# A fused two-block kernel: six modulation products moved among a filter's eight tap steps, and a modulation's row turned between the next step's two products

## The reference, cut to what matters

```
# first block
mod = silu(c) @ mod_w + mod_b                   # 12 pieces of 512 columns
u = a * sigmoid(gt)                             # from h @ w1 + b1
u = causal_dwconv(u, dw_w) + dw_b               # 31 taps, depthwise, 8 tiles of 128 channels
u = silu(layernorm(u)); y = u @ w2 + b2
# second block, needs nothing of the first: its two filters
h = (hdn @ fw3 + fb3).reshape(L, 2, 2, 512)     # hdn: 1024 x 64
h = h * exp(-t * deltas)
hk = rfft(concat([h_fwd, 0, h_bwd reversed]))   # as a product with a table "filt"
```

## Time and profile before

| | |
|---|---|
| median of 3 runs | 3297.73 us (3294.17 to 3299.56) |
| the profiled execution | 3292.07 us, its span 3290.3 us |
| PE busy | 3096.4 us, 94% of the span |
| DVE busy | 1712.3 us, 52% |
| ACT, POOL busy | 1011.6 us, 399.8 us |
| stretch of the list `OTHER` | about 245 to 464 us of the span |

### The profile page before, as it was taken

The page is one execution under the profiler, slowest core; times in us unless marked ns, Lnnn a source line. Parts: engine busy times, 40 slices in busy tenths (PEclk is TensorE's granted clock), DMA queues, the critical chain, the costliest instruction groups (busy, mean ns, idle before and its releaser), DMA issues. The chain is left out here.

```text
span 3290.3 us, 33491 instructions
## 1 busy us (share of the span) xinstructions
PE 3096.4 (94%) x13786; PEld 2499.5 (76%) x13786; DVE 1712.3 (52%) x1776; ACT 1011.6 (31%) x1203; POOL 399.8 (12%) x161
## 2 busy tenths in 40 slices
PE   7998869899999999989999999899999999999996
PEld 3784357788888888778888877677877788888885
DVE  5697786656556554574511076577455322223225
ACT  3454444332222122233221133476222311111111
POOL 0595550000000000000200034000110000000000
PEclk9998879899999999899999999999998999999998
DMA  6114423132223331321432343531331202112112
GB/s 207 58 33 159 148 96 113 73 109 64 90 77 116 100 100 63 109 77 64 141 113 92 108 154 128 136 74 50 126 118 56 76 26 64 49 38 62 38 45 109
DMA packets 96192, 301.24 MB, mean 92 GB/s; under 512 B 11205, under 2 KB 15045, under 8 KB 95847
## 3 DMA queue, kind: packets, MB, share of 16 engines
q1 hardware_dynamic: 96040, 299.09, 27.8%
HBM read 251.34 MB, written 47.71 MB: 91 GB/s over the span
## 5 line engine op out<-in xcount | busy, mean ns | idle before, releaser
L708 PE MATMUL ps<-mainr,wh 128*128 128x512 f32 (+1 forms) x6592 | 1782.0, 390 | 29.5 <-issue 12.7
L708 PEld LDWEIGHTS ps<-mainr,wh 128*128 128x128 f32 x6592 | 1238.6, 189 | 286.6 <-issue 31.2
L708 PE MATMUL ps<-mainr,wl 128*128 128x512 f32 (+1 forms) x3296 | 1030.7, 389 | 0.0
L708 PEld LDWEIGHTS ps<-mainr,wl 128*128 128x128 f32 x3296 | 623.1, 189 | 128.6
L1713 DVE TENSOR_TENSOR wl<-raw,wh 128x1024 fp32r<-128x1024 f32 (+2 forms) x272 | 294.1, 1083 | 457.1 <-ACT wh L1235 456.9
L1235 ACT CAST wh<-raw 128x1024 fp32r<-128x1024 f32 (+2 forms) x320 | 282.0, 886 | 746.9 <-PE ps L708 538.3
L1972 DVE TENSOR_TENSOR mainf<-mainf,ps 128x1024 f32<-128x1024 f32 x80 | 97.7, 1221 | 215.0 <-PE ps L708 215.0
L754 PE MATMUL ps<-mainr,wh 128*128 128x512 f32 x576 | 164.4, 409 | 36.0 <-issue 21.8
L2013 DVE SCALAR_TENSOR_TENSOR ps<-mainf,vec,ps 128x1024 f32<-128x1024 f32 (+1 forms) x174 | 180.9, 1102 | 2.5 <-ACT ps L1424 2.3
L2497 POOL TENSOR_TENSOR tmp<-tmp,mainf 128x1024 f32<-128x1024 f32 x8 | 27.5, 3444 | 1160.6 <-DMA mainf<-in_rope 1097.5
L1049 PE MATMUL ps<-mainr,wh 128*128 128x512 f32 x512 | 160.3, 395 | 6.3 <-POOL wl L2464 6.1
(11 more groups left out here) (236 smaller groups left out, 2896.8 us busy)
## 6 DMA issues: line engine op xcount, KB each, us to landing
raw<-in_mod_w SPq DMA_DIRECT2D x48, 512.0 KB, 4.5
raw<-in_ada_w SPq DMA_DIRECT2D x48, 512.0 KB, 3.7
raw<-in_f_up SPq DMA_DIRECT2D x44, 512.0 KB, 4.2
raw<-in_g_up SPq DMA_DIRECT2D x44, 512.0 KB, 3.5
raw<-in_w_in SPq DMA_DIRECT2D x40, 512.0 KB, 4.1
raw<-in_pw SPq DMA_DIRECT2D x24, 512.0 KB, 3.6
sc_x<-mainf SPq DMA_DIRECT2D x24, 512.0 KB, 2.6
mainf<-sc_x SPq DMA_DIRECT2D x24, 512.0 KB, 6.2
```

What stands on the lines that cost most here:

```text
L708: ins = e.matmul(out, wt[:, a:b], xs[n], start=kk == 0 and t == 0, stop=kk == kt - 1 and t == 2)
```

## The change

In the list, the modulation pieces come behind steps 0, 3 and 5 of each filter instead of 3, 5 and 7. On PE and DVE, the turn and the bias add are done inside the next tap step: between the products of its two banks, and between the two "dec". Nothing is added or taken away.

```diff
     for s in range(32):
         out.append(("f", s))
-        if s % 16 < 8 and s % 2 == 1 and s not in (1, 17):
+        if s % 16 in (0, 3, 5):
             out.append(next(mods))
...
-    def filter_step(s):
+    def filter_step(s, turn):
...
                 e.matmul(k.BANK("taps", o, step, n), m.ex[0:65, 128 * step:128 * step + 128],
                          m.mf[0:65, 3 * SLOT + c0:3 * SLOT + c0 + 512], start=True, stop=True).then_inc(*k.to("taps", o, step, n))
+                if turn and n == 0:
+                    modulation_turn(*turn)
...
     for kind, s in OTHER:
-        if turn:
-            modulation_turn(*turn)
+        if kind == "f":
+            filter_step(s, turn)
             turn = None
-        if kind == "f":
-            filter_step(s)
...
                 e.tensor_tensor(t, t, dec, ALU.mult).then_inc(*k.to("dec", o, step, n))
+                if row and n == 0:
+                    modulation_add(*row)
...
     for kind, s in OTHER:
-        if row:
-            modulation_add(*row)
+        if kind == "f":
+            filter_step(s, row)
             row = None
-        if kind == "f":
-            filter_step(s)
```

More of the change, by code:

```diff
@@ L2041, in filter_pairs, with filter_step @@
         e.scalar_tensor_tensor(out=b, in0=b, scalar=-2.0, in1=f, op0=ALU.mult, op1=ALU.add).then_inc(*k.to("fw3d", 1))
-    def filter_step(s):
+    def filter_step(s, row):
         o, step = s // 16, s % 16
```

## The result

The changed kernel took 3281.99 us (median of 10 runs, 3277.29 to 3293.38), the kernel before, beside it, 3293.82 us (10 runs, 3290.13 to 3299.56). The ratio is 0.9964 [0.9956, 0.9972]: 11.9 us faster, with an interval of 9 to 14.5. The forecast of 3282.5 holds, and the likeliest case came true. The sum behind it was 15.2 us.

What follows compares the result with a forecast made beforehand. DVE was taken to bound the kernel through its waits before 410; gains of 6.2 us (first filter) and 9.0 (second) sum to 15.2, giving 3282.5 from the median 3297.7. Range 3276 to 3296, the forecast's own 3278 to 3288.

Steps and rivals of the forecast that it cites:

- the likeliest case: Whole kernel: 15.2 us less waiting, to 3282.5 us from the median; chance 70%.
- DVE is what bounds the stretch: In the list, DVE sets the length: each microsecond of its waiting removed before 410 should shorten the kernel.
- no change: Rival: product steps or POOL's additions set both filters' time, so waits only change place: 3297; chance 9%.
- the slower one: Rival: half clock stays through all modulations, 14.1 us each; 16 us slower than before, about 3313; chance 9%.
- part of the gain is lost: Rival: closer packing brings more slow DVE splits beside POOL, 6.3 us in one filter, about 3289; chance 12%.
- The product step moves off the path: First filter: first product step runs beside DVE's steps 6 and 7, ending 301.5 at half clock against 307.0 before.
- First modulation, step 0: First filter, behind step 0: length 8.9 us, step 1's convolution at 259.2 instead of 255.85; cost 3.35 us.
- a wait near 3 us: Sign of being right: DVE's wait for the first turned row in the first filter, near 3 us.
- Second, step 3: Behind step 3, likewise in the second filter: length 8.9 us, cost is length less 4.9, so 4.0 us.
- Third, step 5: Behind step 5, likewise in the second filter: length 7.03 us, casts end 9.3 us after its start; cost 1.9 us.
- Second filter's first modulation hidden: Behind step 16: runs 346.8 to 353.8 while DVE is busy until 356.9; cost 0.3 us.
- at nothing: Other orders of decay loads on SP, and POOL's work: no cost; a late load would cost a few us, once.

Runs made afterwards that it cites:

- short modulations: Changed kernel with seven of eight matmuls in each of the six modulations taking 4 columns instead of 512; 3275.53 us, 0.9941 of before.
- the row ahead: Changed kernel with modulation weights asked for ahead of the decay table, row copied ahead of casts, splits behind the next tap step; 3281.42 us, 0.9959 of before.
- the places alone: Kernel before with modulations behind steps 0, 3 and 5, turn and bias add still ahead of the next step; 3288.01 us (0.9977), again 3283.87.
- turn alone: Changed kernel with modulations back behind steps 3, 5 and 7, turn and add staying ahead of a product step; 3292.30 us (0.9986), again 3292.94 (0.9998).

## Why the prediction was right, and which of its steps was wrong

*DVE is what bounds the stretch.* Right: A is 4.4 and B 5.1 us shorter, and C and what ends the list followed (L811 from 476.32 to 468.23; from step 0 on, 10.2 earlier). DVE's waits behind 411 before were 0.6 us and not the 0.3 read from the earlier trace rows, for a wait of 0.3 ahead of a split at 414.04 was left out; nothing hangs on it. The rival "no change" is out, and so is the slower one: no whole modulation took 14 us (7.03 to 9.90 without a wait for weights). The rival "part of the gain is lost" is nearly out. C is no longer than before, and the three slow splits in it took 3.15, 3.36 and 2.30 us where they had taken 3.17, 3.35 and 2.27. Ahead of the first product step a split now takes 1.80 and 1.72 us (302.43, 401.01) instead of 1.2, about 1 us in all. In one more profile of this kernel another one, at 308.50, took 3.21, but DVE waited less for product steps there (1.0 in all, not 4.7).

*The product step moves off the path.* Right, and it carries the gain: the waits for it fell by 10.3 us. Half clock was taken for the first filter and came; 1.15 us of waiting was left.

*First modulation, step 0.* Forecast 3.35, because I took half clock from the earlier trace rows. It ran in 7.03 here, and the way from the first dec to step 1's convolution grew from 9.84 to 10.80: cost 1.0. The sign "a wait near 3 us" was missed (1.00 + 0.56); another execution of the same kernel had it (D of 9.42, a wait of 3.40, 14.05 for that way: cost 4.2).

*Second, step 3.* Forecast 4.0; D - 4.54 gives 5.2 for 9.76 us, and 4.6 for the second filter's 9.10. Two small errors: the constant, and a D that was longer than the 8.9 taken.

*Third, step 5.* Forecast 1.9, measured 3.6 in the first filter (1.69 + 0.84 of waiting for casts, and 1.10 between the dec beyond the usual 0.60), 2.4 in the second (about 4 there in the two other profiles of this kernel). The step took the casts' end from the earlier trace rows as if it belonged to the modulation; it belongs to the loads. The runs with short modulations and with the row ahead show it.

So in the first filter 1.0 + 5.2 + 3.6 = 9.8 where 9.25 was forecast, and 1.15 of waiting for the product step: 1.7 us lost of 6.2, as A says (1.8).

*Second filter's first modulation hidden.* This is the step that failed. Forecast 0.3; step 16's dec at 347.05 to step 17's convolution at 359.19 is 12.1 us, where 8.8 does when the weights are there: 3.3 (1.8 in the execution that stayed at full clock behind the wait). The cause is what the prediction costed "at nothing", the orders of loads on SP. I had looked at the decay tables in that queue, and not at what stands behind a decay load that waits: the modulation's own weights. In the first filter they are just in time, in the second not: the fourth part is asked for 1.3 us behind the modulation's start there (250.03 against 248.76), and 4.3 us behind it here (348.80 against 344.46), where PE is further ahead of DVE. Shown by the trace, and by taking it away: in the four traces in which SP asks earlier, this way takes 8.77 to 8.79. With 4.6 and 2.4 for the others, the filter costs 10.3 where 6.2 was forecast; B missed by 3.9, since its gain had been rounded down by 0.2.

Sum: 15.2 less 1.8 less 3.9, and 0.7 more in C than foreseen, is the 10.2 measured. That the time came within 1 us of the forecast is in good part luck: the stretch gave 10 to 11 us and not 15.2, and the kernel before ran at 3293.8 beside it, 3.9 below the median from which the forecast started. The signs named in advance show it better than the time. Less the 2.1 us by which step 0 came later, the first L2080 came at 303.3 (forecast 302), the second filter's 9.5 us earlier than before (forecast 15), and the end of the list at 466.2 (forecast 461). DVE waited for no decay table, and for no L2080 above 2 us.

The rule that was weighed against the change, the Trainium skill, "TensorE: Matmul & The Clock Gate", section "HAM oscillation — how this bites in real kernels", holds in part here: PE does begin the modulation behind step 3 slow after waiting, in both filters (9.76 and 9.10 us against 7.03). But it did before as well (8.83 and 8.94). More and smaller batches did not lower the granted clock: over the whole stretch it was 0.86 and 0.84 in the two profiles of before, and 0.87, 0.86 and 0.87 in the three of the changed kernel.

What stays open: how the gain divides. In the first set of runs places and turn alone gave 7.6 and 4.6 us where both gave 10.2; the turn gave 0.7 when run again. By profiles they make 3.7 and 3.5 of 10.9. Some interaction is likely, for with the places alone a late row holds two products and not one (the 1.6 us a filter above), but its size is within the scatter.

## What to carry to other kernels

When work is moved forward in a list, follow each of its inputs back through the queue that asks for it: a load that stands behind a waiting issue comes late however early its buffer is free. Work that only has to be done by some time is best put where no other engine's wait stands behind it; here a row's turn cost 0.54 us less between two products than ahead of them. A cost taken from an interval of the trace belongs to what ended that interval, which may be a DMA beside the instruction one looks at. And one profile is not enough for a difference of 3 to 4 us in a stretch of 220: the same kernel differs by as much from one to the next.

## What the runs showed of the hardware

- The same modulation varies by up to 2.4 us from execution to execution. In seven traces of the changed kernel and its near variants the first two of the first filter took 7.03 and 9.76, 9.42 and 8.35, 7.98 and 9.32, 7.03 and 9.81, 7.03 and 9.87, 7.03 and 9.90, 9.33 and 8.31 us. A long first one went with a shorter second one there (sums of 16.8 to 17.8), but not always: one profile of the places alone had 9.41 and 9.78.
- The kernel with less work for PE got a lower clock (mean 0.955 against 0.961 to 0.966 in the other profiles, and in the stretch 0.73 against 0.84 to 0.87 in the profiles of before and changed). Its tap steps' products took 2.08 us a pair instead of 1.12, so part of what it saved went there; how much of the time that is was not measured.
- A weight part asked for at 348.80 was used at 352.57, so this load took at most 3.8 us from its issue, with four more issued behind it.
- A split on DVE that started 0.5 us into an addition of POOL's took 2.9 us, and 1.2 alone; why it does was not tested.
